# Norms of the attention heads: block sums on every partition in one matmul, roots and reciprocals on whole tiles

## The chip, the cores and the metric

The kernel runs on one core of one Trainium2 chip. The metric is the device time of one execution in microseconds, as the median of several runs. TensorE, VectorE, ScalarE, GpSimd and SyncE each have their own queue of instructions and wait for each other through semaphores.

## The reference

Two transformer blocks run one after the other over 256 latent tokens and 256 context tokens of width 1024, each with two layers. The kernel numbers them as layers 0 to 3. Layers 0 and 1 have a gated chunk mixer (a), a windowed attention with eight heads of 64 (b) and a differential attention with four heads of twice 32 (c). Layer 2 has a grouped attention with eight query and two key heads of 128, layer 3 a pooling mixer. A convolutional feed-forward part follows in each. What matters here is the norm that each head's queries and keys get right after the projection, and the rotation behind it:

```python
def rms_norm(x, gain=None):
    xf = x.astype(jnp.float32)
    y = xf * lax.rsqrt(jnp.mean(xf * xf, axis=-1, keepdims=True) + EPS)
    if gain is not None:
        y = y * gain.astype(jnp.float32)
    return y.astype(x.dtype)
...
q_b = apply_rope(rms_norm(bq.reshape(b, l, B_HEADS, B_HEAD_DIM), b_qnorm[i]), cos_b, sin_b)
k_b = apply_rope(rms_norm(bk.reshape(b, l, B_KV_HEADS, B_HEAD_DIM), b_knorm[i]), cos_b, sin_b)
...
q_c = rope_maps(rms_norm(cq.reshape(b, l, C_HEADS, 2, C_QK_DIM), c_qnorm[i]), cos_c, sin_c)
...
return rmsnorm(q, g_q), rmsnorm(k, g_k), v
```

The mean runs over the 64, 32 or 128 channels of a head. Everything is computed in f32.

## The kernel before, in words

Activations lie with channels on the partitions and tokens along the free dimension. Every weight block (128 output channels, 1024 inputs) is loaded by SyncE's queue into one of four `RAW` tiles. ScalarE copies it to a reduced-precision high part `WHI` (`hi_split`, L736), and VectorE subtracts to get the low part `WLO` (`lo_split`, L1223). TensorE multiplies high by high, high by low and low by high (`products`, L1981 to L1983; `products_tok`, L2029 to L2031, for the v blocks, which come out with tokens on the partitions). Both splits of block n+4 are queued in the slot of block n (`ahead`).

The projection of a layer (`proj(l)` in each engine's program) is a loop of slots, one per tile of output. Layer 0 has 17 tiles, layer 1 has 16, layer 2 has 12. `QS` is the slot of the first query or key tile: 4, 3 and 0. Of such tiles (`qk_names`) layers 0 and 1 have nine, in the order ck0, ck1, cq0, cq1, bk, bq0 to bq3, and layer 2 ten, k0, k1, q0 to q7. They are followed by the bv tiles (four, three blocks each, of which the last is done inside the attention) or by the two v tiles of layer 2. In layer 0 all nine have 512 tokens. In layer 1 ck0, ck1 and bk have 512 and the others 256; in layer 2 the two k tiles have 512 and the q tiles 256.

A query or key tile q, whose products are made in slot QS + q, then goes through these steps. The lists of `lagged` (L468) say in which slot each is queued.

- ScalarE squares it out of PSUM into `SQ` (L887) and copies it with the head's gain (L888), which frees the bank.
- `sums(q)`, TensorE, a slot later (L2176 to L2186): for each 128 tokens one f32 matmul with the squares as weights and a thin matrix of ones (`blk64`, `blk32` or `ones`: 2, 4 or 1 columns) as the moving side. The sums come out with tokens on the partitions, one column per head, in `STAT`.
- ScalarE takes the roots of these 2 to 16 columns into `SM` (L905), and VectorE the reciprocals (L1456).
- In layers 0 and 1 GpSimd copies each reciprocal along the row, 64 or 32 times, into `RE` (`spread`, L641 to L652). In layer 2 a broadcast operand does this.
- `spread(q)`, TensorE, three slots after the tile (two in layer 2; L2188 to L2200): transposes of 128x128 (turns) bring the reciprocals into `RB`, so that each channel's partition has its head's factor for each token.
- VectorE multiplies the tile by `RB` (L1447). The rotation (`rope`, L1422 to L1430) has been done before, a slot after the tile: a shuffle, two multiplies and an add of 256 columns, on the first 256 tokens.

In layers 0 and 1 ScalarE then splits the c tiles (L870) and VectorE their low part (L1439); SyncE's queue stacks them. `gated_mix(b)` on TensorE, in the slots QS + 10 and QS + 11, and `gated(b)` on VectorE behind it belong to the a mixer and use `STAT` again. Layer 0's projection also has a unit of the modulation on TensorE in each slot (`mod_unit`, L2089), whose 1 MB of weights GpSimd's queue fetches into the homes `GWA` and `GWB` (`unit`, L610 to L616). GpSimd's queue also loads the tables (`tables`, L626): `TAB` holds the cosines, sines and masks. In each engine's program the order of the work is the order of the code.

The attention of layer 2 begins on TensorE with a wait for the tenth `qnorm` (L2413). That of layers 0 and 1 (`weave`) begins with the stacked c tiles and waits for the ninth `qnorm` before its second step. The lag list reads:

```python
def lagged(l, slot):
    nqk, slot = len(qk_names[l]), slot - QS[l]
    return [q if 0 <= q < nqk else None for q in (slot - 1, slot - (3 if IS_L[l] else 2))]
```

Of the kernel before, what the change touches and what calls it, by code (L numbers as in the profile page):

```python
# [22 lines left out]
ALU = mybir.AluOpType  # L23
# [3 lines left out]
P = 128  # L27
# [96 lines left out]
LT = {"c64": 0, "s64": 256, "c32": 512, "s32": 768, "mask0": 1024, "mask1": 1152}  # L124
ST = {"c128": 0, "s128": 256}
# [9 lines left out]
def total(per, l):  # L135
    return sum(per[:l])
# [25 lines left out]
def build(nc, A):  # L162
    ctx = ExitStack()
    with ctx:
# [84 lines left out]
        TAB = sb("TAB", [P, 1280], at=w0 + 77824)  # L249
# [19 lines left out]
        def sem(name):  # L269
# [20 lines left out]
        qsq, qstat, qrs, qrr, qre, qrb, qnorm, qrope, chain = (  # L290
            sem("qsq"), sem("qstat"), sem("qrs"), sem("qrr"), sem("qre"), sem("qrb"), sem("qnorm"), sem("qrope"),
            sem("chain"))
# [161 lines left out]
        NSLOT = [max(TPROJ[l], QS[l] + len(qk_names[l]) + 3) for l in range(3)]  # L454
# [13 lines left out]
        def lagged(l, slot):  # L468

            nqk, slot = len(qk_names[l]), slot - QS[l]  # L470
            return [q if 0 <= q < nqk else None for q in (slot - 1, slot - (3 if IS_L[l] else 2))]
# [135 lines left out]
        def _(gp):  # L607
# [18 lines left out]
            def tables(l):  # L626
# [9 lines left out]
                elif l == 2:  # L636
                    gp.dma_start(TAB[:, 0:512], A["tab_s"]).then_inc(tab_in[l], 16)
                else:
                    gp.dma_start(EDGE[:].rearrange("p a b c -> p (a b c)"), A["edge"]).then_inc(tab_in[l], 16)

            def spread(l, q):  # L641

                col, _, _ = scols[l]
                _, nh, nt, _ = qk_kind(l, qk_names[l][q])
                c = 120 + col[qk_names[l][q]]
                k = total([9, 9, 10], l) + q
                gp.wait_ge(qrr, k + 1)
                if q >= 2:
                    gp.wait_ge(qrb, k - 1)
                gp.tensor_copy(RE[:, q % 2, 0:nt * P].rearrange("p (a b) -> p a b", b=P // nh),  # L650
                               SM[:, c:c + nt * nh].unsqueeze(2).broadcast_to((P, nt * nh, P // nh))
                               ).then_inc(qre, 1)  # L652

            def proj(l):
                for i in range(NSLOT[l]):
                    if l == 0 and 1 <= i < 15:
                        unit(1 + (i + 1) // 8, (i + 1) % 8)
                    root, _ = lagged(l, i)
                    if root is not None:
                        spread(l, root)  # L660
# [22 lines left out]
            proj(0)  # L683
# [15 lines left out]
            proj(1)  # L699
# [28 lines left out]
        def _(act):  # L728
# [131 lines left out]
            def proj(l):  # L860
# [3 lines left out]
                for i in range(NSLOT[l]):  # L864
# [34 lines left out]
                    if root is not None:  # L899

                        name = qk_names[l][root]
                        kind, nh, nt, _ = qk_kind(l, name)
                        c, w = col[name], nh * nt
                        act.wait_ge(qstat, nq + root + 1)
                        act_f(SM[:, c:c + w], STAT[:, c:c + w], ACT.Sqrt, scale=1.0 / {"b": 64, "c": 32, "s": P}[kind],  # L905
                              bias=epsc).then_inc(qrs, 1)
# [303 lines left out]
        def _(dve):  # L1210
# [178 lines left out]
            def proj(l):  # L1389
# [42 lines left out]
                for i in range(NSLOT[l]):  # L1432
# [9 lines left out]
                    if norm_q is not None:  # L1442
                        nt = qk_kind(l, names[norm_q])[2]
                        dve.wait_ge(qrb, nq + norm_q + 1)
                        dve.wait_ge(qrope, nq + norm_q + 1)
                        x = qk_tile(l, norm_q)[:, 0:nt * P]
                        v.tensor_tensor(x, x, RB[:, 0:nt * P], ALU.mult).then_inc(qnorm, 1)  # L1447
# [522 lines left out]
        def _(pe):  # L1970
# [199 lines left out]
            def proj(l):  # L2170
# [5 lines left out]
                def sums(q):  # L2176

                    kind, nh, nt, _ = qk_kind(l, names[q])
# [580 lines left out]
```

## Time and profile before

| what | value |
|---|---|
| median of 3 runs (lowest, highest) | 1581.37 us (1580.14, 1584.23) |
| the profiled execution, its own time | 1582.11 us |
| its span | 1580.0 us |
| TensorE (PE) busy | 1514.3 us, 96% |
| VectorE (DVE) busy | 1105.2 us, 70% |
| ScalarE (ACT) busy | 836.5 us, 53% |
| GpSimd (POOL) busy | 95.0 us, 6% |
| chain that ended last, by engine | PE 71%, DVE 14%, issue 5%, ACT 5%, DMA 3% |

The profile is of one execution. The span runs from the first to the last instruction that it records; 2.1 us of the execution's time lie around it. A busy share is an average over stages: the projections of layers 0, 1 and 2 take 83, 48 and 41 us of the span, and the rest is attention, output projection and feed-forward parts. In the chain a piece of work is counted from what released it to what it released, so an instruction that overlaps the one before it shows less there than its own duration. f32 matmuls with two real operands are recorded as two passes.

### The profile page before, as it was taken

How to read it: one execution, taken by the hardware profiler on the slowest of the kernel's cores; microseconds unless marked ns; L12 is line 12 of the kernel's file. 1: busy time of each engine (PE TensorE's matmuls, PEld its weight loads, DVE VectorE, ACT ScalarE, POOL GpSimd, SP SyncE). 2: the span in 40 equal slices, each digit the busy share in tenths (PEclk: the TensorE clock that was granted, in tenths of full speed). 3: DMA queues.
4: the chain of work that ended last, by engine and by line, in shares of the span. 5: the costliest groups of instructions: out<-in, count | busy, mean ns of one | idle time of the engine just before them, and what ended most of it. 6: DMA issues, size and time to landing. Idle time of an engine off the chain costs nothing.

```text
span 1580.0 us, 27185 instructions
## 1 busy us (share of the span) xinstructions
PE 1514.3 (96%) x9444; PEld 1270.5 (80%) x9444; DVE 1105.2 (70%) x1986; ACT 836.5 (53%) x1526; POOL 95.0 (6%) x160
## 2 busy tenths in 40 slices
PE   4999999999999999999999999999999998799997
PEld 2777667688888888887789998998788886588886
DVE  4464874797786467686678876774588855778865
ACT  3442882544444322465756664546566644566653
POOL 0011000110100011010000000000000000000000
PEclk9999999999999999999999999999999999799999
DMA  9775105665632488453177645542756587446563
GB/s 375 275 238 199 41 2 213 216 222 188 207 125 82 161 260 285 131 150 97 41 262 260 196 146 157 185 135 93 280 163 191 171 310 273 170 133 185 178 187 115
DMA packets 79685, 288.27 MB, mean 182 GB/s; under 512 B 9280, under 2 KB 12864, under 8 KB 71664
## 3 DMA queue, kind: packets, MB, share of 16 engines
q1 hardware_dynamic: 61056, 190.23, 37.5%
q0 software_dynamic: 18544, 96.90, 17.2%
q8 instruction: 54, 0.88, 0.2%
q14 instruction: 31, 0.25, 0.0%
HBM read 283.16 MB, written 1.05 MB: 180 GB/s over the span
## 4 chain that ended last, share of the span: by engine, by line
PE 71%; DVE 14%; issue 5%; ACT 5%; DMA 3%; DVEq 1%; SPq 0%; ACTq 0%
PE B L1981 15%; PE B L1983 14%; PE B L1982 14%; DVE WLO L1223 6%; PE B L2008 5%; PE B L2018 3%; PE B L2037 3%; PE B L2281 2%; DVE Y L1698 2%; DMA MW<-in_wmod 1%; ACT WHI L736 1%; PE B L2304 1%; DVE Y L1711 1%; PE B L2029 1%; PE B L2031 1%
## 5 line engine op out<-in xcount | busy, mean ns | idle before, releaser
L1223 DVE TENSOR_TENSOR WLO<-RAW,WHI 128x1024 fp32r<-128x1024 f32 (+1 forms) x376 | 412.2, 1101 | 151.5 <-ACT WHI L736 150.7
L736 ACT ACTIVATE WHI<-RAW 128x1024 fp32r<-128x1024 f32 (+1 forms) x376 | 357.0, 957 | 140.8 <-PE B L1983 86.6
L1981 PE MATMUL B<-HHL,WHI 128*128 128x256 f32 (+1 forms) x1184 | 397.2, 336 | 8.7 <-DVE HHL L1896 2.7
L1983 PE MATMUL B<-HHL,WLO 128*128 128x256 f32 (+1 forms) x1184 | 391.4, 331 | 0.0
L1982 PE MATMUL B<-HHL,WHI 128*128 128x256 f32 (+1 forms) x1184 | 391.3, 330 | 0.0
L1981 PEld LDWEIGHTS B<-HHL,WHI 128*128 128x128 f32 x1184 | 224.9, 190 | 42.6 <-issue 17.3
L1983 PEld LDWEIGHTS B<-HHL,WLO 128*128 128x128 f32 x1184 | 224.8, 190 | 21.1
L1982 PEld LDWEIGHTS B<-HHL,WHI 128*128 128x128 f32 x1184 | 225.1, 190 | 19.8
L2008 PE MATMUL B<-HHL,WHI 128*128 128x512 f32 x672 | 168.6, 392 | 0.0
L2008 PEld LDWEIGHTS B<-HHL,WHI 128*128 128x128 f32 x672 | 121.0, 189 | 21.6
L2008 PE MATMUL B<-MID,WHI 128*128 128x512 f32 x462 | 124.4, 399 | 4.1 <-ACT WHI L736 3.6
L2008 PEld LDWEIGHTS B<-MID,WHI 128*128 128x128 f32 x462 | 82.0, 191 | 19.4 <-ACT WHI L736 3.7
L2018 PEld LDWEIGHTS B<-HHL,WLO 128*128 128x128 f32 x672 | 91.7, 190 | 6.6
L2018 PE MATMUL B<-HHL,WLO 128*128 128x256 f32 x672 | 93.7, 282 | 0.0
L1689 DVE SCALAR_TENSOR_TENSOR Y<-B,VEC,Y 128x510 f32<-128x510 f32 (+1 forms) x88 | 54.0, 614 | 56.6 <-ACT Y L1084 44.1
L1981 PE MATMUL B<-MID,WHI 128*128 128x512 f32 (+1 forms) x264 | 91.4, 346 | 0.0
L1982 PE MATMUL B<-MID,WHI 128*128 128x512 f32 (+1 forms) x264 | 91.1, 345 | 0.0
L1983 PE MATMUL B<-MID,WLO 128*128 128x512 f32 (+1 forms) x264 | 91.0, 345 | 0.0
L1077 ACT ACTIVATE Y<-Y 128x256 f32<-128x256 f32 (+1 forms) x88 | 41.5, 472 | 90.8 <-DVE Y L1714 47.8
L1088 ACT ACTIVATE MID<-Y 128x256 f32 (+3 forms) x88 | 41.5, 471 | 82.4 <-DVE Y L1732 53.1
L2018 PEld LDWEIGHTS B<-MID,WLO 128*128 128x128 f32 x462 | 67.0, 191 | 7.3
L2018 PE MATMUL B<-MID,WLO 128*128 128x256 f32 x462 | 69.0, 283 | 0.0
(273 smaller groups left out, 2262.1 us busy)
## 6 DMA issues: line engine op xcount, KB each, us to landing
RAW<-in_wup SPq DMA_DIRECT2D x176, 512.0 KB, 3.8
GWR<-in_wmod POOLq DMA_DIRECT2D x27, 1024.0 KB, 8.1
RAW<-in_wdn SPq DMA_DIRECT2D x64, 384.0 KB, 3.3
RAW<-in_wproj SPq DMA_DIRECT2D x44, 512.0 KB, 4.6
RAW<-in_wdn SPq DMA_DIRECT2D x64, 320.0 KB, 3.2
WDU<-in_wdot POOLq DMA_DIRECT2D x32, 512.0 KB, 5.0
WDD<-in_wdot POOLq DMA_DIRECT2D x32, 512.0 KB, 4.7
GWA<-in_wmod POOLq DMA_DIRECT2D x15, 1024.0 KB, 5.7
```

Of the source, the lines that this page charges most:

```text
L736: act_f(WH[s][:, 0:kts, :], RAW[s][:, 0:kts, :], ACT.Copy).then_inc(hi_done, 1)
L1077: act_f(yg, yg, ACT.Silu).then_inc(silu_done, 1)
L1088: act_f(mid, yv if isinstance(i, int) else Y[:, 2 * j + 1:2 * j + 2, 0:t], ACT.Copy).then_inc(mid_hi, 1)
L1223: v.tensor_tensor(WL[s][:, 0:kts, :], RAW[s][:, 0:kts, :], WH[s][:, 0:kts, :].bitcast(F32), ALU.subtract).then_inc(lo_done, 1)
L1689: v.scalar_tensor_tensor(out=y[:, :, 1:256], in0=b[:, :, 0:255], scalar=w(0, which), in1=y[:, :, 1:256], op0=ALU.mult, op1=ALU.add).then_i ...
L1698: v.tensor_tensor(Y[:, s0 + k, 256:512], banks[s0 + k][:, 0:256], Y[:, s0 + k, 256:512], ALU.add).then_inc(drained, 1)
L1981: mm(bank[:, 0:t], wh, a, start=first and k == ks[0], stop=False)
L1982: mm(bank[:, 0:t], wh, b, start=False, stop=False)
L1983: ins = mm(bank[:, 0:t], wl, a, start=False, stop=stop and k == ks[-1])
L2008: return mm(bank[:].rearrange("p (a b) -> p a b", a=2), WH[s][:, k, :], T[:, :, k0 + k, 0:256], start=first and k == 0, stop=stop and k == ...
L2018: mm(bank[:, 0:256], WL[s][:, k, :], T[:, 0, k0 + k, 0:256], start=False, stop=False)
L2037: ins = mm(GB[32 * j:32 * j + 32, :], CV[:, 4 * kt:4 * kt + 32], W[:, j, :], start=kt == 0, stop=kt == 7)
```

## The change

Three 128x128 matrices of ones and zeros are added to the loaded tables: `same64` and `same32` (ones where two channels belong to the same head) for layers 0 and 1, and `all` (only ones) for layer 2. `sums(q)` becomes one f32 matmul with this block matrix as weights and all 256 or 512 columns of squares as the moving side. The sum of each head comes out on every one of its partitions, in `RB`. ScalarE takes the root of the whole tile from `RB` into `RE`, and VectorE takes the reciprocal of the whole tile in place, waits for it, and multiplies. TensorE's spreads, GpSimd's copies, the small roots and the small reciprocals go. The multiply comes two slots after the tile in all layers. GpSimd fetches the modulation's units of layer 0 without steps between them, and in layer 1 waits for `dotted` instead of running its copies.

```diff
-LT = {"c64": 0, "s64": 256, "c32": 512, "s32": 768, "mask0": 1024, "mask1": 1152}
-ST = {"c128": 0, "s128": 256}
+LT = {"c64": 0, "s64": 256, "c32": 512, "s32": 768, "mask0": 1024, "mask1": 1152, "same64": 1280, "same32": 1408}
+ST = {"c128": 0, "s128": 256, "all": 512}
...
-        TAB = sb("TAB", [P, 1280], at=w0 + 77824)
+        TAB = sb("TAB", [P, 1536], at=w0 + 77824)
...
-        NSLOT = [max(TPROJ[l], QS[l] + len(qk_names[l]) + 3) for l in range(3)]
+        NSLOT = [max(TPROJ[l], QS[l] + len(qk_names[l]) + 2) for l in range(3)]
...
-            return [q if 0 <= q < nqk else None for q in (slot - 1, slot - (3 if IS_L[l] else 2))]
+            return [q if 0 <= q < nqk else None for q in (slot - 1, slot - 2)]
...
-                    gp.dma_start(TAB[:, 0:512], A["tab_s"]).then_inc(tab_in[l], 16)
+                    gp.dma_start(TAB[:, 0:640], A["tab_s"]).then_inc(tab_in[l], 16)
...
-            def spread(l, q):
-
-                col, _, _ = scols[l]
-                _, nh, nt, _ = qk_kind(l, qk_names[l][q])
-                c = 120 + col[qk_names[l][q]]
-                k = total([9, 9, 10], l) + q
-                gp.wait_ge(qrr, k + 1)
-                if q >= 2:
-                    gp.wait_ge(qrb, k - 1)
-                gp.tensor_copy(RE[:, q % 2, 0:nt * P].rearrange("p (a b) -> p a b", b=P // nh),
-                               SM[:, c:c + nt * nh].unsqueeze(2).broadcast_to((P, nt * nh, P // nh))
-                               ).then_inc(qre, 1)
-
-            def proj(l):
-                for i in range(NSLOT[l]):
-                    if l == 0 and 1 <= i < 15:
-                        unit(1 + (i + 1) // 8, (i + 1) % 8)
-                    root, _ = lagged(l, i)
-                    if root is not None:
-                        spread(l, root)
+            def first_units():
+                for i in range(1, 15):
+                    unit(1 + (i + 1) // 8, (i + 1) % 8)
...
-            proj(0)
+            first_units()
...
-            proj(1)
+            gp.wait_ge(dotted, 64)
...
                         act.wait_ge(qstat, nq + root + 1)
-                        act_f(SM[:, c:c + w], STAT[:, c:c + w], ACT.Sqrt, scale=1.0 / {"b": 64, "c": 32, "s": P}[kind],
-                              bias=epsc).then_inc(qrs, 1)
+                        if nq + root >= 2:
+                            act.wait_ge(qnorm, nq + root - 1)
+                        act_f(RE[:, root % 2, 0:nt * P], RB[:, 0:nt * P], ACT.Sqrt,
+                              scale=1.0 / {"b": 64, "c": 32, "s": P}[kind], bias=epsc).then_inc(qev, 1)
...
-                        dve.wait_ge(qrb, nq + norm_q + 1)
+                        dve.wait_ge(qev, nq + norm_q + 1)
                         dve.wait_ge(qrope, nq + norm_q + 1)
                         x = qk_tile(l, norm_q)[:, 0:nt * P]
-                        v.tensor_tensor(x, x, RB[:, 0:nt * P], ALU.mult).then_inc(qnorm, 1)
+                        re = RE[:, norm_q % 2, 0:nt * P]
+                        link(v.reciprocal(re, re))
+                        v.tensor_tensor(x, x, re, ALU.mult).then_inc(qnorm, 1)
...
-                    if root is not None:
-                        _, nh, nt, _ = qk_kind(l, names[root])
-                        c = col[names[root]]
-                        dve.wait_ge(qrs, nq + root + 1)
-                        v.reciprocal(SM[:, 120 + c:120 + c + nh * nt], SM[:, c:c + nh * nt]).then_inc(qrr, 1)
...
                     pe.wait_ge(qsq, nq + q + 1)
+                    if q == 0:
+                        pe.wait_ge(tab_in[l], 48 if IS_L[l] else 16)
                     if nq + q:
-                        pe.wait_ge(qrs, nq + q)
-                    w = {"b": cst("blk64", 0, 2), "c": cst("blk32", 0, 4), "s": cst("ones")}[kind]
-                    for t in range(nt):
-                        c = col[names[q]] + nh * t
-                        ins = mm(STAT[:, c:c + nh], SQ[:, q % 2, P * t:P * t + P], w, start=True, stop=True)
-                    ins.then_inc(qstat, 1)
-
-                def spread(q):
-
-                    if IS_L[l]:
-                        pe.wait_ge(qre, nq + q + 1)
-                    else:
-                        pe.wait_ge(qrr, nq + q + 1)
-                    if q:
-                        pe.wait_ge(qnorm, nq + q)
-                    for t in range(qk_kind(l, names[q])[2]):
-                        c = 120 + col[names[q]] + t
-                        r = RE[:, q % 2, P * t:P * t + P] if IS_L[l] else SM[:, c:c + 1].broadcast_to((P, P))
-                        ins = nc.tensor.transpose(RB[:, P * t:P * t + P], r, ident)
-                    ins.then_inc(qrb, 1)
+                        pe.wait_ge(qev, nq + q)
+                    c = {"b": LT["same64"], "c": LT["same32"], "s": ST["all"]}[kind]
+                    mm(RB[:, 0:nt * P], TAB[:, c:c + P], SQ[:, q % 2, 0:nt * P], start=True, stop=True).then_inc(qstat, 1)
...
-                        pe.wait_ge(qrs, nq + 9)
...
-                    if spr is not None:
-                        spread(spr)
```

## Rows read from the trace of the kernel before

**Rows 1.** Busy us of each engine in four stretches; last: granted clock, DMA share, GB/s.
```profile
81.38:127.70 46.32, 46.32 (x262) 35.36 (x261) 27.89 (x57) 18.81 (x33) 10.03 (x12) 1.00 0.75 235
70.40:153.70 83.30, 82.83 (x500) 63.65 (x498) 44.24 (x87) 29.30 (x53) 16.65 (x20) 1.00 0.69 220
680.20:728.50 48.30, 46.89 (x341) 44.45 (x341) 36.03 (x87) 24.62 (x51) 10.45 (x10) 1.00 0.52 159
1019.50:1060.60 41.10, 40.51 (x347) 40.28 (x348) 32.19 (x80) 19.85 (x41) 0.00 (x0) 1.00 0.47 151
```
**Rows 2.** Timeline of VectorE, layers 0 and 2: start us, us, instruction, idle before it.
```profile
80.23 1.22 DVE L1223 TENSOR_TENSOR WLO<-RAW,WHI 128x1024 fp32r<-128x1024 f32 x1
...
84.70 2.00 DVE L1223 TENSOR_TENSOR WLO<-RAW,WHI 128x1024 fp32r<-128x1024 f32 x1 [0.69 <-ACT WHI L736]
...
1023.43 0.68 DVE L1447 TENSOR_TENSOR SQK<-SQK,B 128x512 f32<-128x512 f32 x1
...
1030.32 0.42 DVE L1447 TENSOR_TENSOR SQK<-SQK,B 128x256 f32<-128x256 f32 x1
...
1030.67 0.45 DVE L1427 STREAM_SHUFFLE NT<-SQK 128x256 f32<-128x256 f32 x1
...
1032.36 1.20 DVE L1223 TENSOR_TENSOR WLO<-RAW,WHI 128x1024 fp32r<-128x1024 f32 x1
1033.80 0.42 DVE L1447 TENSOR_TENSOR SQK<-SQK,B 128x256 f32<-128x256 f32 x1 [0.23 <-PE B L2199]
```
**Rows 3.** Chain of waits in the projections: start us, us, work.
```profile
129.54 0.79 PE B L2185 x8
...
131.32 0.59 PE B L2199 x4
...
150.62 0.59 PE B L2199 x4
...
712.39 0.44 PE B L2029
...
1053.77 0.27 PE B L2199 x2
...
1059.79 0.23 PE B L2199 x2
1060.04 0.43 DVE SQK L1447
...
1063.96 0.86 PE B L2419 x2
```
**Rows 4.** Groups by line and form: count, then busy us, mean ns, idle before.
```profile
L1456 DVE RECIPROCAL SM<-SM 128x8 f32<-128x8 f32 x8 | 1.6, 196 | 0.0
L1456 DVE RECIPROCAL SM<-SM 128x16 f32<-128x16 f32 x6 | 1.5, 249 | 7.7 <-ACT SM L905 7.7
L1456 DVE RECIPROCAL SM<-SM 128x2 f32<-128x2 f32 x8 | 1.3, 158 | 0.0
L1456 DVE RECIPROCAL SM<-SM 128x4 f32<-128x4 f32 x6 | 1.0, 170 | 0.0
L1407 DVE RECIPROCAL SM<-SM 128x16 f32<-128x16 f32 x1 | 0.2, 193 | 0.0
L1407 DVE RECIPROCAL SM<-SM 128x8 f32<-128x8 f32 x1 | 0.2, 153 | 0.0
L1447 DVE TENSOR_TENSOR QC<-QC,B 128x512 f32<-128x512 f32 x6 | 4.1, 688 | 13.9 <-PE B L2199 13.8
L1447 DVE TENSOR_TENSOR SQK<-SQK,B 128x256 f32<-128x256 f32 x8 | 3.4, 421 | 8.1 <-PE B L2199 8.1
L2419 PE MATMUL B<-SQK 128*128 128x512 f32 x32 | 16.1, 596 | 0.6 <-DVE SQK L1447 0.6
```
**Rows 5.** Timeline of VectorE in layer 1, columns as in rows 2.
```profile
687.08 0.44 DVE L1427 STREAM_SHUFFLE NT<-QC 128x256 f32<-128x256 f32 x1
...
696.40 0.69 DVE L1447 TENSOR_TENSOR QC<-QC,B 128x512 f32<-128x512 f32 x1 [0.54 <-PE B L2199]
```

More of the change, by code:

```diff
@@ L289, in build @@
                                                          sem("mid_hi"), sem("mid_lo"))
-        qsq, qstat, qrs, qrr, qre, qrb, qnorm, qrope, chain = (
-            sem("qsq"), sem("qstat"), sem("qrs"), sem("qrr"), sem("qre"), sem("qrb"), sem("qnorm"), sem("qrope"),
-            sem("chain"))
+        qsq, qstat, qev, qnorm, qrope, chain = (sem("qsq"), sem("qstat"), sem("qev"), sem("qnorm"), sem("qrope"),
+                                                sem("chain"))
         vn_ready, amix, amul, a_hi, bfc = sem("vn_ready"), sem("amix"), sem("amul"), sem("a_hi"), sem("bfc")
@@ L901, in proj @@
                         name = qk_names[l][root]
-                        kind, nh, nt, _ = qk_kind(l, name)
-                        c, w = col[name], nh * nt
+                        kind, _, nt, _ = qk_kind(l, name)
                         act.wait_ge(qstat, nq + root + 1)
-                        act_f(SM[:, c:c + w], STAT[:, c:c + w], ACT.Sqrt, scale=1.0 / {"b": 64, "c": 32, "s": P}[kind],
-                              bias=epsc).then_inc(qrs, 1)
+                        if nq + root >= 2:
+                            act.wait_ge(qnorm, nq + root - 1)
+                        act_f(RE[:, root % 2, 0:nt * P], RB[:, 0:nt * P], ACT.Sqrt,
+                              scale=1.0 / {"b": 64, "c": 32, "s": P}[kind], bias=epsc).then_inc(qev, 1)
                         if root == len(qk_names[l]) - 1:
@@ L2176, in sums @@
                 def sums(q):
-                    kind, nh, nt, _ = qk_kind(l, names[q])
+                    kind, _, nt, _ = qk_kind(l, names[q])
                     pe.wait_ge(qsq, nq + q + 1)
+                    if q == 0:
+                        pe.wait_ge(tab_in[l], 48 if IS_L[l] else 16)
                     if nq + q:
-                        pe.wait_ge(qrs, nq + q)
-                    w = {"b": cst("blk64", 0, 2), "c": cst("blk32", 0, 4), "s": cst("ones")}[kind]
-                    for t in range(nt):
-                        c = col[names[q]] + nh * t
-                        ins = mm(STAT[:, c:c + nh], SQ[:, q % 2, P * t:P * t + P], w, start=True, stop=True)
-                    ins.then_inc(qstat, 1)
-                def spread(q):
-                    if IS_L[l]:
-                        pe.wait_ge(qre, nq + q + 1)
-                    else:
-                        pe.wait_ge(qrr, nq + q + 1)
-                    if q:
-                        pe.wait_ge(qnorm, nq + q)
-                    for t in range(qk_kind(l, names[q])[2]):
-                        c = 120 + col[names[q]] + t
-                        r = RE[:, q % 2, P * t:P * t + P] if IS_L[l] else SM[:, c:c + 1].broadcast_to((P, P))
-                        ins = nc.tensor.transpose(RB[:, P * t:P * t + P], r, ident)
-                    ins.then_inc(qrb, 1)
+                        pe.wait_ge(qev, nq + q)
+                    c = {"b": LT["same64"], "c": LT["same32"], "s": ST["all"]}[kind]
+                    mm(RB[:, 0:nt * P], TAB[:, c:c + P], SQ[:, q % 2, 0:nt * P], start=True, stop=True).then_inc(qstat, 1)
                 def gated_mix(b):
@@ L2261, in proj @@
                             ins.then_inc(tile_mm, 1)
-                    root, spr = lagged(l, i)
+                    root, _ = lagged(l, i)
                     if root is not None:
@@ L2730, in _layout @@
     m1 = np.where(k < q, -NEG, 0).astype(np.float32)
-    t["tab_l"] = f(np.concatenate([c64, s64, c32, s32, m0, m1], axis=1))
-    t["tab_s"] = f(np.concatenate([a[near] for a in _rope(128)], axis=1))
+    same = [(q // h == k // h).astype(np.float32) for h in (64, 32, P)]
+    t["tab_l"] = f(np.concatenate([c64, s64, c32, s32, m0, m1, same[0], same[1]], axis=1))
+    t["tab_s"] = f(np.concatenate([a[near] for a in _rope(128)] + [same[2]], axis=1))
     t["ws"] = f(i["a_ws"].transpose(0, 3, 1, 2).reshape(2 * P, 4 * P))
```

## The prediction

> **What bounds the kernel now.** I read the page first, then the stretches of the three projections by windows, then the chain of waits inside them and VectorE's timeline, and last the groups by form, for prices. TensorE is busy 96% of the span (table above), so whatever idle time it gets is new time. The change touches the projections of layers 0, 1 and 2 alone. In their windows [rows 1] the reader should hold VectorE against the stretch: 44.2 of 83.3 us in layer 0, but 36.0 of 48.3 in layer 1 and 32.2 of 41.1 in layer 2. The last two are nearly full; only their tails, where TensorE works on the v tiles, have gaps. Layer 2's timeline shows it: a q slot lasts 3.48 us, and VectorE idles 0.23 of it [rows 2].
>
> **What is taken from TensorE.** In layer 0 the sums of a tile hold the chain for 0.79 us and its spread for 0.59; a spread of 256 tokens is 0.27 [rows 3]. The spreads go. The sums become one f32 matmul, 256 or 512 wide. No such matmul with ones was in the trace, but a score of layer 2 has its form (128 rows, 128 columns of weights, 512 wide, f32, recorded as two passes): 0.86 us of the chain [rows 3]. I take 0.86, and half for 256 columns. The bounds are 0.79, as now, and 1.19, twice the 596 ns of a single pass [rows 4]; the chain is nearer, since passes overlap. A tile of layer 0 saves 0.59 + 0.79 - 0.86 = 0.52 us, one of 256 tokens about 0.2.
>
> **What is given to VectorE.** Each tile had a reciprocal of 2 to 16 columns; now it has one of 256 or 512, ahead of its multiply and linked to it. No row is that wide, so its price is the whole question. Line 1456 gives a straight line over four widths: 158, 170, 196, 249 ns for 2, 4, 8, 16 columns [rows 4]; (249 - 158)/14 = 6.5 ns a column over 145 ns. So 512 columns take 3.47 us and 256 take 1.81; with the gap of a link 3.50 and 1.84. Bounds below: line 1407 has 193 and 153 ns for 16 and 8, so 5.0 a column; much lower, the rate of the multiply, (688 - 421)/256 = 1.04 [rows 4]. Above: eight such passes for each column, 8.3. I take 6.5, on which 28 instructions stand.
>
> The Trainium skill ("VectorE: DVE Perf Modes", the walkthrough of the 8-slice pipeline) says that a reciprocal is an iterated divide with a repeat count of 8. Read as eight passes that speaks for reciprocals longer than the rows': the second rival.
>
> **ScalarE and GpSimd.** The root of a few columns becomes one of the whole bank, at most doubling ScalarE's work on a tile's evacuation; it is busy 29.3, 24.6 and 19.9 us of the stretches [rows 1], so this is 0 on the path. Without that cover it would be some 0.3 us a tile, 9 us in all. It also waits for the multiply two tiles back, with the next evacuation and high split queued behind it; in the ledgers below that multiply lies a slot of VectorE earlier, so 0. GpSimd's 18 copies go. In layer 1 its first 1 MB for the modulation is then issued behind the tables, not after the last copy, beside SP's weight loads. DMA is 0.52 busy there, so 0; if a load had to wait for it, 1 MB at the stretch's 159 GB/s is 6.6 us [rows 1]. TensorE's new wait for the tables is met: VectorE's rope of the same tile waited for them too, and showed no idle time for it. The 128 KB more that they carry: 0.
>
> **Layer 0.** The first bv tile begins at 131.32 + 0.59 = 131.9 [rows 3]. Six spreads and eight sums lie ahead of it: 131.9 - 6 x 0.59 + 8 x 0.07 = 128.9. Its low part is made at the end of VectorE's slot 11. Slot 6 began at 81.38, and can begin near 80.2, as the split that started at 80.23 [rows 2] stands behind squares that no longer wait for a small reciprocal. From 81.38 to 127.7 VectorE was busy for 27.9 us [rows 1]. Now six reciprocals (21.0) and, by the shorter lag, a sixth multiply (0.6) join, and six small reciprocals go (1.2), and with GpSimd's copies the delay beside them (0.6; one split that met a copy took 2.00 us where its neighbour took 1.22 [rows 2]): 47.7, done at 127.9, 1.0 us ahead of need. So layer 0 stays TensorE's: 9 x 0.52 = **-4.7 us**. The cover is thin.
>
> **Layer 1.** From 687.08, where slot 5 starts on VectorE, to 712.39, where the first bv tile starts right behind its low split [rows 3, 5], VectorE idled 0.54 us. Into this stretch come six reciprocals, three of 512 (ck0, ck1, bk) and three of 256 (cq0, cq1, bq0): 16.0. The sixth multiply brings 0.35. Six small reciprocals (0.7), the idle 0.54 and about 0.5 of delay beside GpSimd's copies go: +14.6 at the first bv tile. Three later spreads of about 0.25 leave, the sums add 0.1: **+14.0 us** when the scores begin. The last three reciprocals run beside the bv tiles.
>
> **Layer 2.** The attention waits for all ten multiplies; the last ended at 1060.04 + 0.43 = 1060.47 [rows 3]. VectorE's new ledger begins at 1023.34 (the multiply at 1023.43 [rows 2], one small reciprocal less): two k slots of 0.61 + 1.62 + 1.11; six q slots of 0.35 + 1.62 + 1.12 (the starts in [rows 2], the small reciprocal left out); then 1.97 and 0.35 for the two last. Together 27.5, and reciprocals of 2 x 3.50 + 8 x 1.84 = 21.7: done at 1072.6. **+12.1 us**. The v tiles are not the later ones: their low part is there after four q slots, at 1056.7, and two tiles of 1059.79 - 1054.04 = 5.75 [rows 3] and sums of 0.43 end near 1068.7.
>
> Behind both attentions no wait is new, and TensorE, busy throughout, gives nothing back. Sum -4.7 + 14.0 + 12.1 = +21.4 us on the profiled execution's 1582.11; the median, 1581.37, stands 0.7 below it. Forecast 1602.8.
>
> **Rivals.** First, a lower slope for wide operations. At 5.0 ns, 2304 columns in layer 1 and 3072 in layer 2 give back 5376 x 1.5 ns = 8.1 us: 1594.7. For it line 1407, against it the four widths of line 1456.
>
> Second, eight passes a column, 8.3 ns. Layer 1 gets 2304 x 1.8 ns = 4.1 more, layer 2 5.5. In layer 0 VectorE misses the start of bv by 4.6 us, and then delays the second gated mix, which waits for the product behind the ninth multiply, to 154.4, where the mix began at 150.62 + 0.59 = 151.2 [rows 3]: +3.2 in place of -4.7. Together 38.9: 1620.3. For it a whole number of passes, of which a short operation may hide some; against it the same straight line.
>
> Third, **faster**: the slope belongs to short operations, and a wide reciprocal streams like the multiply, 0.69 and 0.42 us. Its one place is VectorE's reciprocal. Layer 0 gives -4.7. Layer 1's bv starts 1.8 late and it ends at +1.2. Layer 2 is TensorE's again, lighter by ten spreads and with its last multiply ahead of its last v tile: -2.7. Sum -6.2: 1575.2. It decides below 6.5 - 21.4/5.4 = 2.5 ns a column. Against it: no reciprocal in the trace is under 5.0.
>
> Fourth, the new matmul costs 1.19 us: layer 0 keeps 3.0 of its gain less, the others are VectorE's and don't move: 1605.8.
>
> **How the numbers follow.** Forecast 0.57 (the fourth rival and small misses of cover within it), first 0.11, second 0.24, third 0.06, near nothing 0.02. 0.3%, 4.7 us, is about what the runs can tell from no change: faster 0.06, same 0.02, slower 0.92. The range reaches from just under the first rival to just over the second, 1593 to 1622.
>
> **What would show it.** Reciprocals of 3.5 and 1.8 us, 14 of each; no GpSimd copy in the projections; TensorE's idle time in layers 1 and 2 ended by VectorE's low splits and, ahead of layer 2's scores, by its multiply, 12 us later within the stage; in layer 0 none, and its scores 4 to 5 us earlier. I am wrong if the wide reciprocal takes under 1.3 us, or if TensorE is busy throughout layers 1 and 2.

## The result, and the profile after

| what | before | after |
|---|---|---|
| median of 4 runs (lowest, highest) | 1580.76 us (1578.03, 1584.23) | 1607.25 us (1604.46, 1608.34) |
| ratio, 95% interval | | 1.0157 (1.014 to 1.0175) |
| profiled execution: time, span | 1582.11, 1580.0 us | 1604.46, 1602.7 us |
| TensorE busy, granted clock | 96%, 0.985 | 95%, 0.978 |
| VectorE busy | 1105.2 us | 1169.3 us |

The kernel is slower by 1.57%, which is some 24.8 us; the two medians lie 26.5 us apart. The forecast was 1602.8, 4.5 us too low, in a range of 1593 to 1622. The new kernel's profiled execution was the fastest of its four, so the profiles show a little less of it, 22.7 us of span.

I measure each stage from the first shuffle of its rotation to the first row minimum of its attention, on VectorE. First the six landmarks of the kernel before (start us, us, instruction, idle before it):

```profile
71.57 0.44 DVE L1427 STREAM_SHUFFLE NT<-QC 128x256 f32<-128x256 f32 x1
155.37 1.29 DVE L1481 TENSOR_REDUCE SM<-B 128x1 f32<-128x512 f32 x2 [0.54 <-PE B L2298]
...
680.23 0.44 DVE L1427 STREAM_SHUFFLE NT<-QC 128x256 f32<-128x256 f32 x1
728.49 1.28 DVE L1481 TENSOR_REDUCE SM<-B 128x1 f32<-128x512 f32 x2
...
1020.61 0.45 DVE L1427 STREAM_SHUFFLE NT<-SQK 128x256 f32<-128x256 f32 x1
1061.74 0.69 DVE L1595 TENSOR_REDUCE SM<-B 128x1 f32<-128x512 f32 x1 [1.28 <-PE B L2419]
```

The same in the changed kernel, with the last two multiplies' neighbourhood and the second and third minimum of layer 2:

```profile
70.69 0.44 DVE L1410 STREAM_SHUFFLE NT<-QC 128x256 f32<-128x256 f32 x1
151.11 1.29 DVE L1461 TENSOR_REDUCE SM<-B 128x1 f32<-128x512 f32 x2 [0.54 <-PE B L2261]
...
675.93 0.44 DVE L1410 STREAM_SHUFFLE NT<-QC 128x256 f32<-128x256 f32 x1
739.18 1.28 DVE L1461 TENSOR_REDUCE SM<-B 128x1 f32<-128x512 f32 x2
...
1032.34 0.45 DVE L1410 STREAM_SHUFFLE NT<-SQK 128x256 f32<-128x256 f32 x1
...
1081.76 1.75 DVE L1431 RECIPROCAL RE<-RE 128x256 f32<-128x256 f32 x1
1083.55 0.43 DVE L1432 TENSOR_TENSOR SQK<-SQK,RE 128x256 f32<-128x256 f32 x1
1085.61 0.69 DVE L1575 TENSOR_REDUCE SM<-B 128x1 f32<-128x512 f32 x1 [1.64 <-PE B L2382]
1087.32 0.69 DVE L1575 TENSOR_REDUCE SM<-B 128x1 f32<-128x512 f32 x1 [1.01 <-PE B L2382]
1088.67 0.69 DVE L1575 TENSOR_REDUCE SM<-B 128x1 f32<-128x512 f32 x1 [0.66 <-PE B L2382]
```

Subtracting gives the stages. Every kernel of this study stands in one table, in the order of the runs; the last column is the ratio to the kernel before, each measured against it on its own chip. The three figures marked * are not comparable with the others, because there the start of the stage moved and not its end; the experiment with the table loaded ahead says why.

| kernel | layer 0 | layer 1 | layer 2 | ratio (95%) |
|---|---|---|---|---|
| before | 83.80 | 48.26 | 41.13 | |
| the change | 80.42 | 63.25 | 53.27 | 1.0157 (1.014 to 1.0175) |
| change in layer 0 alone | 80.42 | 48.43 | 41.13 | 0.998 (0.9971 to 0.9989) |
| reciprocals of 16 columns | 80.42 | 49.04 | 38.89 | 0.9972 (0.9959 to 0.9985) |
| reciprocal root on ScalarE | 80.42 | 47.65 | 40.00 | 0.9989 (0.9976 to 1.0002) |
| change in layer 1 alone | 83.79 | 62.99 | 41.15 | 1.0108 (1.0092 to 1.0125) |
| change in layer 2 alone | 83.80 | 48.24 | 52.92 | 1.0093 (1.0072 to 1.0114) |
| TensorE kept busy | 80.42 | 61.09 | 52.84 | 1.0154 (1.0139 to 1.017) |
| reciprocal roots, table ahead | 80.52 | 44.05* | 38.57* | 0.9975 (0.9963 to 0.9987) |
| more VectorE work in layer 0 | 95.42 | 63.01 | 52.92 | 1.0243 (1.0223 to 1.0262) |
| each layer's best | 80.42 | 49.83 | 38.57* | 0.9977 (0.9966 to 0.9988) |

So the change costs -3.4, +15.0 and +12.1 us in its three stages, 23.7 together, where the whole span is 22.7 longer. The rest lies outside the stages: 0.9 us less ahead of the first, 1.0 more between layer 1's and layer 2's, 1.2 less behind the last. Kernels that have the same code there differ by as much (the last stretch is 518.3 us before and 515.9 with the change in layer 0 alone), so a microsecond or two outside the stages says nothing.

The groups by form of the changed kernel (count, then busy us, mean ns, idle before) hold the prices that the rows before did not show [rows 4]:

```profile
L1431 DVE RECIPROCAL RE<-RE 128x512 f32<-128x512 f32 x14 | 46.9, 3348 | 0.1
L1431 DVE RECIPROCAL RE<-RE 128x256 f32<-128x256 f32 x14 | 24.5, 1747 | 0.2
L1432 DVE TENSOR_TENSOR QC<-QC,RE 128x512 f32<-128x512 f32 x6 | 4.2, 692 | 0.2
L1432 DVE TENSOR_TENSOR SQK<-SQK,RE 128x256 f32<-128x256 f32 x8 | 3.4, 425 | 0.3
...
L888 ACT ACTIVATE RE<-B,CST 128x512 f32<-128x512 f32 x14 | 9.7, 690 | 4.2 <-DVE QC L1432 3.8 <-PE B L2166 0.4
L888 ACT ACTIVATE RE<-B,CST 128x256 f32<-128x256 f32 x14 | 6.6, 474 | 33.7 <-DVE SQK L1432 20.0 <-DVE QKB L1432 7.5 <-DVE QC L1432 6.1
```

The reciprocal costs 3348 - 1747 = 1601 ns more for 256 columns more: 6.25 ns a column, six times the multiply's (692 - 425)/256 = 1.04. ScalarE's roots spend 33.7 us waiting for VectorE's multiplies: VectorE sets the pace.

The windows of the three stages, with the columns of [rows 1], say the same. Against the stretch, VectorE is now at 70.3 of 79.9, 54.5 of 63.3 and 51.7 of 53.3 us, and TensorE is no longer busy throughout in the last two:

```profile
69.50:149.40 79.90, 79.47 (x410) 54.20 (x408) 70.27 (x87) 32.46 (x54) 5.81 (x11) 1.00 0.69 226
675.90:739.20 63.30, 49.44 (x287) 44.02 (x287) 54.52 (x87) 26.95 (x51) 0.00 (x0) 0.87 0.35 105
1031.20:1084.50 53.30, 42.60 (x298) 39.87 (x297) 51.65 (x80) 22.40 (x41) 0.00 (x0) 0.94 0.35 116
```

The last three numbers of a row are the granted clock, the DMA share and GB/s. The clock was 1.00 in all of [rows 1]; here it is 0.87 in layer 1 and 0.94 in layer 2. That is the one thing in these rows that the prediction does not have. TensorE's timeline of layer 1, only the rows with the longer idle times, shows what stands before it:

```profile
701.38 0.67 PE L2166 MATMUL B<-SQ,TAB 128*128 128x256 f32 x2 [3.17 <-ACT RE L888]
...
707.25 0.67 PE L2166 MATMUL B<-SQ,TAB 128*128 128x256 f32 x2 [0.83 <-ACT RE L888]
...
714.32 1.19 PE L2166 MATMUL B<-SQ,TAB 128*128 128x256 f32 x2 [3.54 <-ACT RE L888]
...
721.61 0.69 PE L2009 MATMUL B<-WHI,HHL 128*128 128x384 f32 x1 [6.10 <-DVE WLO L1206]
```

And the windows around the last two of these waits and around layer 2's first scores:

```profile
712.00:716.00 4.00, 1.19 (x2) 0.50 (x2) 3.90 (x8) 2.06 (x4) 0.00 (x0) 0.58 0.25 87
716.00:721.00 5.00, 0.00 (x0) 0.00 (x0) 4.90 (x10) 1.42 (x2) 0.00 (x0) 0.50 0.45 131
721.00:725.00 4.00, 3.39 (x11) 3.39 (x12) 3.90 (x8) 0.00 (x0) 0.00 (x0) 0.50 0.37 131
725.00:730.00 5.00, 5.00 (x26) 4.95 (x25) 4.90 (x9) 1.75 (x3) 0.00 (x0) 0.87 0.36 105
1084.00:1087.00 3.00, 2.88 (x4) 1.19 (x5) 0.69 (x1) 0.66 (x2) 0.94 (x2) 0.62 0.00 0
```

Behind 3.54 and 6.10 us of idle time the first bv tile starts at a granted clock of 0.50, the 1.2 GHz level, and its granted clock is 0.87 over the next window. In this execution layer 2's scores start at 0.62, and their minima stand 1.71 and 1.35 us apart.

### The profile page after: what moved, and what is told of

It reads as the page before. It is cut to its first block and busy times, and to the rows that moved or that the text cites. A ratio compares the mean times of both kernels' runs of the same rounds, so it can differ in the third digit from the quotient of the medians.

```text
span 1602.7 us, 26762 instructions
## 1 busy us (share of the span) xinstructions
PE 1514.7 (95%) x9248; PEld 1256.5 (78%) x9248; DVE 1169.3 (73%) x1986; ACT 845.5 (53%) x1526; POOL 74.1 (5%) x142
## 3 DMA queue, kind: packets, MB, share of 16 engines
HBM read 283.49 MB, written 1.05 MB: 178 GB/s over the span
## 5 line engine op out<-in xcount | busy, mean ns | idle before, releaser
L1431 DVE RECIPROCAL RE<-RE 128x512 f32<-128x512 f32 (+1 forms) x28 | 71.3, 2547 | 0.3
```

Source lines behind the costliest of these rows:

```text
L1431: link(v.reciprocal(re, re))
```

## The experiments

The theory is that VectorE's wide reciprocals make the loss (in layers 1 and 2), while the block matrix itself gains in layer 0. The rivals: that the shorter lag and the new waits behind the multiply cost what the reciprocals seem to; that TensorE's clock has a share of its own; and that the stages lean on each other.

**The change in layer 0 alone.** A list says for each layer whether it takes the new steps or the old ones:

```diff
+NEW = [True, False, False]
...
+            return [q if 0 <= q < nqk else None for q in (slot - 1, slot - (3 if IS_L[l] and not NEW[l] else 2))]
...
+                    if root is not None and not NEW[l]:
+                        spread(l, root)
```

> The change in layer 0 alone, layers 1 and 2 as before. Theory (the cost is the width of VectorE's reciprocal, and layer 0 has room for it): the scores of layer 0 begin 3.4 to 4.7 us earlier and nothing later is slower, 1576.5 against 1580.8 before. Rival (the new waits on one RB bank, roots that wait for the multiply two tiles back, cost TensorE time by themselves): TensorE waits for roots in layer 0 too, and the time is 1580 or more.

Measured: 1576.87 us (11 runs) against 1581.41 (27 runs), ratio 0.998 (0.9971 to 0.9989): by the ratio a gain of 3.2 us, where the medians lie 4.5 apart. Layer 0's stage is 80.42, exactly that of the full change, and the other two are those of before. Layer 0's part of the change is a gain, and this kernel beats both.

**Reciprocals of 16 columns.** The wait, the link and the multiply stay; the reciprocal covers only the first 16 columns of the tile, so that the rest is multiplied by the root instead of its reciprocal.

```diff
-                        link(v.reciprocal(re, re))
+                        link(v.reciprocal(re[:, 0:16], re[:, 0:16]))
```

> The change with VectorE's reciprocal cut to the first 16 columns of the tile, so the other columns are multiplied by the root and the output is not the reference's; every wait, the root of the whole tile and the one matmul stay. Theory (width): about 0.25 us in place of 3.35 and 1.75, 68 us less on VectorE, layers 1 and 2 are TensorE's again and keep its 2 to 3 us each: 1574. Rival (the waits): layers 1 and 2 stay 10 us or more late, 1595 or more.

Measured: 1574.9 us, ratio 0.9972 (0.9959 to 0.9985). The loss is gone: layer 1 falls from 63.25 to 49.04, layer 2 from 53.27 to 38.89. The group of this kernel shows what was taken away, 71.4 us of VectorE's work down to 6.9:

```profile
L1431 DVE RECIPROCAL RE<-RE 128x16 f32<-128x16 f32 x28 | 6.9, 247 | 2.9 <-ACT RE L888 2.7
```

The rival of the new waits falls, since they are all still there. A little of it is left in layer 1, which stays 0.8 us above before; there TensorE waits once for 3.1 us for the low split of the first bv tile, and its granted clock is 0.50 from 708 to 710 us, just behind that wait. Layer 0 does not move at all, so its gain owes nothing to VectorE.

**The reciprocal root on ScalarE.** ScalarE's function is changed and VectorE's reciprocal leaves.

```diff
-                        act_f(RE[:, root % 2, 0:nt * P], RB[:, 0:nt * P], ACT.Sqrt,
+                        act_f(RE[:, root % 2, 0:nt * P], RB[:, 0:nt * P], ACT.Abs_reciprocal_sqrt,
...
-                        link(v.reciprocal(re, re))
```

> The change with ScalarE's reciprocal-root function in place of the root, and no reciprocal on VectorE: one ScalarE instruction a tile does what two engines did. Theory (width on VectorE): as with the thin reciprocal, 1574, with two more table loads of 1.3 us in each of layers 0 and 1 beside TensorE's work. Rival (the waits): 1595 or more. A third possibility is that the function's own rate on ScalarE is low: then ScalarE's instruction lasts over 0.69 us and the roots are late.

Measured: 1578.37 us, ratio 0.9989 (0.9976 to 1.0002), not to be told from before. The root costs the same as the plain one, 689 and 477 ns, and the loss is gone here too. The expected 1574 was not reached: in layer 1 TensorE waits 1.1 us for a root and 1.9 for a low split, and in layer 2 0.9 for a root. Seven loads of ScalarE's function table now stand ahead of roots, where the changed kernel has two; these are the groups:

```profile
L888 ACT ACT_TABLE_LOAD x5 | 6.4, 1283 | 0.1
...
L855 ACT ACT_TABLE_LOAD x2 | 2.6, 1283 | 0.0
```

**The change in layer 1 alone**, by the same list.

```diff
-NEW = [True, False, False]
+NEW = [False, True, False]
```

> The change in layer 1 alone. Theory: the time from layer 1's first rope to its first minima grows by 15 us, as in the whole change (13.4 from VectorE until the first v tile, 2.2 from TensorE's lower clock behind its idle time, 0.6 back from the spreads), 1595.8. Rival (the loss is made of what layer 0 hands on, a later start of loads and splits): much less than 15 when layer 0 is as before.

Measured: 1596.76 us, ratio 1.0108 (1.0092 to 1.0125). Its stage is 62.99, 14.7 above before.

**The change in layer 2 alone.**

```diff
-NEW = [False, True, False]
+NEW = [False, False, True]
```

> The change in layer 2 alone; layers 0 and 1 as before. If the stages add up, layer 2's stage (first rope to first score minimum) is 53.3 us, 12.1 above before's 41.1, the other two are before's 83.8 and 48.3, and the time is 1581 + 12 = 1593 us. A rival, that the stages lean on each other: layer 2's projection starts later in the changed kernel and finds other transfers and another clock, so that alone it costs something else than 12.1, and the three parts (-3.4, +15.0, +12.1) do not sum to the change's +22.7.

Measured: 1594.69 us, ratio 1.0093 (1.0072 to 1.0114). Its stage is 52.92, 11.8 above before. The three parts alone make -3.4, +14.7 and +11.8 in their stages, 23.1 us, where the whole makes 23.7. By more than the 0.6 us that is left, the stages do not lean on each other. Added up, the three ratios give -0.20 + 1.08 + 0.93 = +1.81%, where the whole has 1.57%; with intervals of 0.1 to 0.2% on each of the four that is no contradiction, and no proof either. The stages carry the verdict.

**TensorE kept busy.** Matmuls that nothing reads fill part of TensorE's idle time.

```diff
+            def keep_busy(n):
+                for _ in range(n):
+                    mm(STAT[:], TAB[:, 0:P], TAB[:, 0:512], start=True, stop=True)
...
+                    if (l, i) == (1, 12):
+                        keep_busy(6)
...
+                    if (l, i) == (1, 11):
+                        keep_busy(3)
...
                 pe.wait_ge(drained, TBASE[l] + TPROJ[l])
+                keep_busy(2)
                 pe.wait_ge(qnorm, nq + len(qk_names[l]))
```

> The changed kernel, with matmuls that nothing reads (TAB by TAB, 512 columns of 4 bytes) put on TensorE where it waits for VectorE: three ahead of the sums and six ahead of the first bv tile in layer 1, two ahead of layer 2's attention. Theory clock: part of what the change costs is TensorE at its lower level just behind those waits. Then the granted clock of the first bv tile's first five us goes from 0.50 to 1.00, its matmuls stand 0.17 apart instead of 0.32 from the start, layer 1's stage falls from 63.25 to about 61.1 and layer 2's first three score minima stand 0.86 apart; the time falls by 2 to 4 us, to about 1603 to 1605. Rival: the clock is a by-product without a price, since VectorE sets the end of both stages; then layer 1's stage stays at 63 and the time at 1607, or rises by what the extra matmuls delay.

The windows of this kernel at the same places:

```profile
712.00:716.00 4.00, 3.04 (x9) 1.38 (x8) 3.90 (x8) 1.84 (x4) 0.00 (x0) 1.00 0.43 149
716.00:721.00 5.00, 4.60 (x11) 1.71 (x9) 4.90 (x10) 1.64 (x3) 0.00 (x0) 1.00 0.50 131
721.00:725.00 4.00, 2.92 (x17) 2.92 (x18) 3.93 (x7) 0.00 (x0) 0.00 (x0) 1.00 0.44 122
725.00:730.00 5.00, 5.00 (x30) 4.95 (x29) 4.90 (x9) 2.39 (x4) 0.00 (x0) 1.00 0.36 111
1084.00:1087.00 3.00, 3.00 (x20) 2.35 (x20) 1.44 (x4) 2.97 (x7) 0.50 (x1) 1.00 0.93 322
```

The clock is 1.00 throughout. TensorE's timeline of this kernel has the first bv tile start 722.08 - 676.41 = 45.67 us into the stage, where it was 721.61 - 675.93 = 45.68 in the changed kernel:

```profile
722.08 0.44 PE L2009 MATMUL B<-WHI,HHL 128*128 128x384 f32 x1 [1.49 <-DVE WLO L1206]
722.36 0.34 PE L2010 MATMUL B<-WLO,HHL 128*128 128x384 f32 x1
722.54 0.34 PE L2011 MATMUL B<-WHI,HHL 128*128 128x384 f32 x1
```

It starts at the same place and its matmuls stand 0.17 to 0.28 apart from the first on, where they stood 0.32 to 0.49 apart, and the stage is 61.09 us instead of 63.25. So 2.2 us of layer 1's loss are the clock. The low clock recurs: the kernel with layer 1 alone and the one with more VectorE work in layer 0, which have no extra matmuls in layer 1, also show 0.50 at the first bv tile, and stages of 62.99 and 63.01.

In layer 2 this run does not show the same. Its first scores are at 1.00 and its minima 0.86 apart, and by the fourth minimum, counted from the stage's start, it is 1.7 us ahead of the changed kernel. But two kernels with the changed kernel's layer 2 and no extra matmul in it have that too. Here are three us from the first score on, with layer 2 alone and with more VectorE work in layer 0:

```profile
1072.00:1075.00 3.00, 3.00 (x9) 1.34 (x10) 1.59 (x3) 1.12 (x3) 1.47 (x3) 1.00 0.30 41
1102.00:1105.00 3.00, 3.00 (x9) 1.34 (x10) 1.53 (x3) 1.06 (x3) 1.42 (x3) 1.00 0.27 38
```

Their stages are 52.92, against 52.84 here. In them TensorE idles 1.1 us ahead of the scores, in the changed kernel 2.46. So the low clock at layer 2's scores belongs to one profiled execution, and the extra matmuls are not shown to have removed it. The span is 3.0 us shorter (1599.7), of which 1.05 lie in the long stretch between layers 1 and 2. The ratio, 1.0154 (1.0139 to 1.017), is too coarse to show a part of this size, and by the runs alone it would be nothing; the stages carry this verdict.

**Reciprocal roots with the table loaded ahead.** ScalarE's reciprocal root again, and these edits besides:

```diff
+                    if i == (QS[l] - 1 if IS_L[l] else 0):
+                        warm(ACT.Abs_reciprocal_sqrt)
...
-                        act_f(SM[:, 104:104 + TT[l] // 32], SM[:, 240:240 + TT[l] // 32], ACT.Sqrt, scale=1.0 / 64,
+                        act_f(SM[:, 104:104 + TT[l] // 32], SM[:, 240:240 + TT[l] // 32], ACT.Abs_reciprocal_sqrt, scale=1.0 / 64,
...
-                    link(v.reciprocal(SM[:, 224:224 + 4 * n], SM[:, 104:104 + 4 * n]))
```

> The changed kernel without any VectorE reciprocal in the projections: every root there (query, key and av means) is ScalarE's Abs_reciprocal_sqrt, and its table is loaded ahead, behind the last Gelu of layers 0 and 1 and at the first tile of layer 2. In the first run of this kind seven table loads of 1.28 us stood between roots, and TensorE waited 1.1 us in layer 1 and 0.9 in layer 2 for them and 1.9 for a low split. If these were the loads, the stages become 80.4, about 46.5 and 38.9, and the time 1574 to 1576 (before 1581, the change in layer 0 alone 1576.9). Rival: the loads were beside the path and layer 1's waits are VectorE's; then layer 1 stays at 47.7 and layer 2 at 40.0, and the time at 1578.

Measured: 1576.76 us, ratio 0.9975 (0.9963 to 0.9987). The time came out a little above the expected 1574 to 1576. The table's 44.05 for layer 1 and 38.57 for layer 2 mislead, because the starts of these stages moved. ScalarE's timeline of layer 1 shows why:

```profile
673.81 1.28 ACT L820 ACT_TABLE_LOAD   x1
...
675.21 1.99 ACT L718 ACTIVATE WHI<-RAW 128x1024 fp32r<-128x1024 f32 x2
```

The load stands ahead of two high splits that VectorE's low splits wait for, and the first shuffle is queued behind these. TensorE's last wait for a low split in front of the load is a landmark that the load cannot move. These are the waits ahead of layers 1 and 2, first in the kernel with the reciprocal root and its loads between the roots, then in this one:

```profile
659.96 0.39 PE L2008 MATMUL B<-WHI,HHL 128*128 128x256 f32 x1 [1.94 <-DVE WLO L1206]
1014.74 0.39 PE L1960 MATMUL B<-HHL,WHI 128*128 128x256 f32 x1 [0.66 <-DVE WLO L1206]
...
662.08 0.39 PE L2009 MATMUL B<-WHI,HHL 128*128 128x256 f32 x1 [1.94 <-DVE WLO L1208]
1013.54 0.39 PE L1961 MATMUL B<-HHL,WHI 128*128 128x256 f32 x1 [0.66 <-DVE WLO L1208]
```

From there to the first minimum:

| kernel | layer 1 | layer 2 |
|---|---|---|
| before | 65.07 | 43.95 |
| reciprocals of 16 columns | 65.84 | 41.71 |
| reciprocal root on ScalarE | 64.44 | 42.81 |
| reciprocal roots, table ahead | 62.36 | 42.91 |
| each layer's best | 66.65 | 42.91 |

So the theory holds in layer 1, which is 2.1 us shorter than with the loads between the roots: the wait of 1.1 us for a root is gone and the one for the low split is 1.2 instead of 1.9. In layer 2 the rival is right. TensorE still waits 1.0 us for the first root, and with the load in either place the stretch is 1.1 to 1.2 us longer than with the plain root and thin reciprocals. Loading ahead at the first tile hides nothing there. Layer 1's gain is hard to see in the time because this execution is 2.7 us slower between layer 0's first minimum and 662.08 than the kernel with the loads between the roots (510.91 against 508.25), in feed-forward work that the edit does not touch; why is not known.

**More VectorE work in layer 0.** One more reciprocal of 256 columns a tile, which nothing reads.

```diff
+                        if l == 0:
+                            link(v.reciprocal(NT[:, norm_q % 2, 256:512], re[:, 0:256]))
                         link(v.reciprocal(re, re))
```

> The changed kernel, with one more reciprocal of 256 columns (1.75 us) on VectorE for each of layer 0's nine tiles, which nothing reads. It measures layer 0's cover. VectorE is busy 7.42 of each tile's 7.52 us in the changed kernel and its split for the first bv tile is 3 us early. Theory: the cover is those 3 us in all and 0.1 to 0.2 a tile; some eight tiles of 1.75 come to 14, less 3 to 4: layer 0's stage goes from 80.4 to about 91 and the time to 1617 or 1618. Rival: TensorE sets the pace there with 3 us to spare on every tile; then the stage stays at 80.4 and the time at 1607.

Measured: 1620.45 us, ratio 1.0243 (1.0223 to 1.0262). Layer 0's stage is 95.42, +15.0, where nine reciprocals of 1.75 are 15.75. That does not make the cover 0.75 us, because part of the 15.0 is not VectorE's. TensorE's timeline, its two long waits alone, and windows of this kernel show it:

```profile
137.67 0.69 PE L2011 MATMUL B<-WHI,HHL 128*128 128x384 f32 x1 [6.78 <-DVE WLO L1206]
...
161.12 1.98 PE L2179 MATMUL B<-WST,AV 128*64 128x128 f32 x16 [2.87 <-DVE AU L1403]
```

```profile
129.00:137.00 8.00, 1.90 (x11) 0.23 (x9) 7.86 (x10) 2.81 (x4) 0.53 (x1) 0.75 0.66 229
137.00:142.00 5.00, 4.33 (x14) 4.33 (x14) 4.93 (x4) 0.00 (x0) 0.00 (x0) 0.50 0.31 105
...
161.00:163.00 2.00, 1.88 (x16) 1.58 (x16) 0.07 (x1) 0.00 (x0) 0.00 (x0) 0.50 0.93 393
```

The first bv tile waits 6.8 us for its low split, close to the six reciprocals ahead of it less the 3.9 that this split was early in the changed kernel (6 x 1.75 - 3.9 = 6.6). Then TensorE is at 0.50 again, and the second gated mix waits 2.9 us more for VectorE's product. In the changed kernel that product is ready at 143.06 and the mix starts at 146.88, so the cover is 3.8 us there too. Here the mix starts 161.12 - 72.64 = 88.48 us into the stage, where it was 146.88 - 70.69 = 76.19: 12.3 us later, which is the added work less the cover. The other 2.7 us of the 15.0 lie behind the mix, in work that TensorE does at 0.50 (the mix takes 1.98 us instead of 1.09). My expectation had the cover about right; it left out the ninth reciprocal and this clock.

**Each layer's best.** The list again, layers 0 and 2 new, with the reciprocal root in layer 2.

```diff
+NEW = [True, False, True]
...
+                    if (l, i) == (2, 0):
+                        warm(ACT.Abs_reciprocal_sqrt)
...
+                                  ACT.Abs_reciprocal_sqrt if l == 2 else ACT.Sqrt,
...
-                            link(v.reciprocal(re, re))
+                            if l != 2:
+                                link(v.reciprocal(re, re))
```

> Each layer takes the form that did best so far: layer 0 the change as made, layer 1 as before, layer 2 the block matrix with ScalarE's Abs_reciprocal_sqrt (table loaded at the first tile) and no VectorE reciprocal. If the stages add up: 80.4, 48.3 and 38.6 us, that is 3.4 + 2.5 us below before's, and the time is about 1575 (ratio 0.9963), 2 us below the change in layer 0 alone. Rival: layer 2's gain is given back behind the stage (the transfers of its next weights set the pace there, as in the runs whose next stretch was 1 us longer); then the time is 1577, the same as with layer 0 alone.

Measured: 1577.33 us, ratio 0.9977 (0.9966 to 0.9988). The time is that of layer 0 alone; this kernel, the one before the last and the change in layer 0 alone cannot be told apart by their times. Layer 2's 38.57 is the misleading figure again: from TensorE's landmark it is 42.91 against 43.95, a gain of 1.0 us and not 2.6. With layer 0's 3.4 that makes 4.4 us, and the ratio says 3.6 (1.9 to 5.4), so no gain has to be given back behind the stage, and the rival is not needed. The profiled execution was the slowest of its twelve, with layer 1's stage 1.6 us longer than before and the two stretches behind it 2.6 and 1.6.

## Why the prediction was right, and where it was off

**The sign and the place** were right. VectorE ends layers 1 and 2, layer 0 stays TensorE's and gains, and with the wide reciprocals taken away the loss is gone. One of the signs was different: TensorE's idle time was to be ended by low splits and by the last multiply. The low splits end 6.1 us of it in layer 1 and 1.4 in layer 2, but ScalarE's roots end 7.8 and 6.8. These roots waited for VectorE's multiplies, so VectorE is still what sets the pace, and with thin reciprocals TensorE has no wait for a root in either layer.

**The reciprocal's price**, on which "28 instructions stand", was read off four widths of 2 to 16 columns as 6.5 ns a column, 3.47 and 1.81 us. It measured 6.25, 3.35 and 1.75. A line from four short rows held over a factor of 32 in width, to 4%. The first rival (5.0) and the third (the reciprocal streams) are out. The second, eight passes a column at 8.3 ns, is out as well. The Trainium skill ("VectorE: DVE Perf Modes", the walkthrough of the 8-slice pipeline) gives the divide a repeat count of 8; by the measured rows a column of the reciprocal costs six of the multiply's, so that number is not its price in columns.

**The new matmul** was the term that was mis-sized in layer 0. "I take 0.86", from the step between two scores. In the changed kernel the tile period is that of ScalarE's squares:

```profile
104.13 0.60 ACT L869 ACTIVATE SQ<-B 128x512 f32<-128x512 f32 x1 [3.29 <-PE B L1963]
...
111.65 0.60 ACT L869 ACTIVATE SQ<-B 128x512 f32<-128x512 f32 x1 [3.78 <-PE B L1963]
```

It is 7.52 us, and before it was 105.52 - 97.67 = 7.85 at the same two tiles. Of the 0.59 + 0.79 = 1.38 us taken away, 0.33 remain as gain, so by difference the matmul costs 1.05 us, not 0.86, though inside the bounds of 0.79 and 1.19. On TensorE's timeline it holds the engine from 103.93 to 104.88, 0.95 us; the other 0.1 is in the spread, whose leaving gave less than the 0.59 of the chain. Over nine tiles the stage gives 3.4 us, 0.38 a tile, where "-4.7" was forecast. It goes the fourth rival's way, by 1.3 of its 3.0 us. Why the matmul is dearer than a score was not tried; a score stands beside others of its kind, a sum between products of another.

**The cover in layer 0.** "The cover is thin", 1.0 us, was computed at the first bv tile. There it is 3.9: the low split ends at 124.97 and the tile starts at 128.88. At the second gated mix, which the forecast took only for the second rival, it is 3.8. The verdict (TensorE's) was right with more room than forecast: within the stage the tile starts 0.9 us later than computed and the low split ends 2.0 earlier, of which the cheaper reciprocals are 0.7. The rest of the 2.0 is not explained.

**Layer 1**: +15.0 for +14.0. At the first bv tile it is +13.5 (45.68 against 712.39 - 680.23 = 32.16), for a forecast of +14.6; the cheaper reciprocals explain 0.5 of that. The low clock then adds 2.2, and the spreads behind it take off 0.7 where 0.6 was forecast. The two misses, -1.1 and +2.2, cancel in part, and that the total is near is partly luck.

**Layer 2**: +12.1 for +12.1. The last multiply ends 1083.98 - 1032.34 = 51.6 us into the stage, for a forecast of 1072.6 - 1020.61 = 52.0. What the cheaper reciprocals gave, the low clock at the scores took back in this execution; the two other kernels with the same layer 2 and no low clock there have 52.92, +11.8. That the two figures meet exactly is luck.

**The step that failed** is the one that says "behind both attentions no wait is new, and TensorE, busy throughout, gives nothing back". It takes TensorE's work after a wait at the price of the rows before, all of which stand at a granted clock of 1.00. In layer 1 the waits of 3.54 and 6.10 us were followed by work at 0.50, which cost 2.2 us of the 22.7; the run that kept TensorE busy took the low clock away, and the 2.2 us with it. In layer 2 the wait of 2.46 us was followed by scores at 0.62, 1.7 us by the fourth minimum, but in this execution alone. Not every low stretch costs: behind layer 1's wait of 3.17 us the clock was 0.50 from 703 to 705 us, but TensorE then waited twice more for VectorE's work, so that stretch was probably off the path; no run tries it alone.

The wait for the table and the issue of GpSimd's transfers were costed at nothing, and the timelines show no wait for them; layer 0's projection has one wait of TensorE, 0.7 us for a row of the modulation, as before. The longer roots were costed at nothing too. In layers 1 and 2 TensorE did wait for them, but the run with thin reciprocals, which has the same roots, has no such wait.

## What to carry to other kernels

Spreading a per-head scalar by a matmul before the root turns a reciprocal of 16 columns into one of 512, and on VectorE it then costs 3.35 us instead of 0.25: move the reciprocal to where the data is narrow, or give it to ScalarE with the root, and count the load of that function's table: it cost layer 2 about 1 us here. The same change is worth taking in a stage that TensorE bounds and not in one where VectorE is at three quarters, so decide it stage by stage. When a change makes TensorE wait a few us, price not only the wait but also the work just behind it, which ran at a granted clock of 0.50 in layer 1 here. And check a landmark before you subtract it: a stage whose first row moved looks shorter than it is.

## What the runs showed of the hardware that was not expected

- VectorE's reciprocal keeps its slope from 2 to 512 columns: 158, 249, 1747 and 3348 ns for 2, 16, 256 and 512.
- ScalarE's Abs_reciprocal_sqrt costs 0.69 us for 512 columns and 0.48 for 256, as the plain root does, but has a table of its own: each change costs 1283 ns.
- TensorE's granted clock was 0.50 from 716 to 721 us, when TensorE was idle, and still from 721 to 725 us, with TensorE at work again; matmuls that nothing reads kept it at 1.00 over the same stretch. It can also fall only after the work has resumed: behind the wait that ended at 701.38 it was 1.00 from 698 to 701 us and 0.50 from 703 to 705.
- The same code can meet it or not: layer 2's first scores ran at 0.62 behind 2.46 us of idle time in one execution and at 1.00 behind 1.1 us in two others.
- A low split beside one of GpSimd's copies took 2.00 us where its neighbour took 1.22 [rows 2]. In the changed kernel, without these copies, all nine low splits from 70 to 150 us take 1.22 or 1.23. This is only observed; no run takes the copies alone away.
